# A two-layer hybrid backbone on one core: half-depth query projections first, and an expert's second step in front of its loops

## What is computed

```python
mod_x = silu(c) @ w_ada[l] + b_ada[l]            # 6 x 1024: shift, scale, gate, twice
mod_c = silu(c_ctx) @ w_ada[l] + b_ada[l]
px = (x * (1 + sc1) + sh1) @ w_in[l]             # and the same for ctx with mod_c
f, q, k, v, g = split(px)                        # 256, 512, 512, 512, 512 columns
mix = concat(fourier_mix(f), diff_attention(rope(q), rope(k), v), chunk_sgu(g))
x = layernorm(ALPHA * x + g1 * (mix @ w_out[l]))
hx = x * (1 + sc2) + sh2
gates = route(hx)                                # 2 of 16 experts for each token
y = sum over e: gates[e] * ((silu(hx @ w1[e]) * (hx @ w3[e])) @ w2[e])
x = layernorm(ALPHA * x + g2 * y)
```

## Time and profile before

| what | value |
|---|---|
| median of 3 runs | 1263.22 us (1261.59 to 1272.76) |
| the profiled execution | 1269.81 us, span of its instructions 1268.0 us |
| mean granted TensorE clock | 0.908 of full |
| TensorE busy | 1025.1 us, 81% of the span |
| DVE, ACT, POOL busy | 336.0, 227.2, 257.6 us |
| moved by DMA | 331.40 MB, mean 261 GB/s |
| waits of `up` for expert weights | 64.9 us |
| of the chain of waits | PE 66%, DMA 16%, issue 9% |

### The profile page before, as it was taken

One profiled execution on the slowest core, in us unless ns is written; L12 is line 12 of the kernel. 1 busy time (PEld: TensorE's weight loads), 2 busy tenths in 40 slices (PEclk: granted clock), 3 DMA queues, 4 the chain that ended last, 5 costly groups with the idle time before them and its releaser, 6 DMA issues.

```text
span 1268.0 us, 24266 instructions
## 1 busy us (share of the span) xinstructions
PE 1025.1 (81%) x9133; PEld 567.7 (45%) x9134; DVE 336.0 (26%) x787; ACT 227.2 (18%) x559; POOL 257.6 (20%) x483
## 2 busy tenths in 40 slices
PE   4999998899999989978775769998997748745860
PEld 1544756444645545544342434555444425423430
DVE  1002217423433212111110146116233201110114
ACT  0211117501411101101010123116122001100100
POOL 1000000100064333332221320000001313312431
PEclk9799999899899999998797859999997879988995
DMA  9993310380647666688999997321876999999952
GB/s 297 407 409 143 133 67 1 120 312 1 265 168 268 235 230 236 232 309 331 350 361 401 387 367 271 115 84 67 300 315 246 370 404 399 381 391 406 387 189 101
DMA packets 91140, 331.40 MB, mean 261 GB/s; under 512 B 12828, under 2 KB 15068, under 8 KB 66516
## 3 DMA queue, kind: packets, MB, share of 16 engines
q1 hardware_dynamic: 68532, 282.13, 58.4%
q0 software_dynamic: 21088, 47.48, 10.7%
q10 hardware_dynamic: 1472, 1.12, 0.3%
HBM read 303.17 MB, written 27.53 MB: 261 GB/s over the span
## 4 chain that ended last, share of the span: by engine, by line
PE 66%; DMA 16%; issue 9%; DVE 4%; ACT 3%; SPq 2%; POOL 0%; POOLq 0%; DVEq 0%; ACTq 0%
PE PS L1632 18%; PE PS L1434 17%; DMA W<-in_moe_w 13%; PE PS L1648 8%; PE PS L1551 7%; PE PS L1380 3%; PE PS L1622 3%; PE PS L1399 2%; DMA W<-in_w_ada 2%; PE PS L1640 2%; PE PS L1601 1%; ACT EX L789 1%; DMA H<-y_rows,DEST 1%; PE PS L1370 1%; PE PS L1562 1%
## 5 line engine op out<-in xcount | busy, mean ns | idle before, releaser
L1632 PE MATMUL PS<-W,EX 128*32 128x256 f32 x4224 | 280.4, 422 | 114.3 <-DMA W<-in_moe_w 64.9
L1632 PEld LDWEIGHTS PS<-W,EX 128*32 128x32 f32 x4224 | 151.3, 121 | 222.2 <-issue 153.3
L1434 PE MATMUL PS<-W,XT 128*128 128x512 f32 (+1 forms) x544 | 219.8, 565 | 3.1 <-ACT XT L722 3.1
L1434 PEld LDWEIGHTS PS<-W,XT 128*128 128x128 f32 x544 | 104.4, 194 | 112.7 <-issue 110.3
L1648 PE MATMUL PS<-W,AT 128*32 128x256 f32 x2112 | 131.0, 389 | 1.5 <-DVE AT L1267 1.5
L692 ACT ACTIVATE AT<-EX 64x512 f32<-64x512 f32 x64 | 40.4, 631 | 446.8 <-PE PS L1622 442.5
L1260 DVE COPY EX<-PS 128x256 f32<-128x256 f32 x66 | 28.0, 425 | 342.7 <-PE PS L1632 342.7
L588 POOL TENSOR_TENSOR RSTD<-VAR,HALF 128x1 f32<-128x1 f32 (+1 forms) x24 | 16.3, 683 | 482.1 <-DVE VAR L968 482.1
L619 POOL DMA_DIRECT2D y_rows<-AT x136 | 67.5, 499 | 207.9 <-DVE AT L1270 198.2
L619 POOL DMA_DIRECT2D y_rows<-EX x128 | 63.5, 496 | 166.2 <-DVE EX L1270 145.7
L1551 PE MATMUL PS<-W,XT 128*128 128x512 f32 x192 | 85.0, 603 | 0.0
(11 more groups left out here) (192 smaller groups left out, 842.3 us busy)
## 6 DMA issues: line engine op xcount, KB each, us to landing
W<-in_moe_w SPq DMA_DIRECT2D x96, 2048.0 KB, 14.1
W<-in_w_ada SPq DMA_DIRECT2D x24, 2048.0 KB, 14.6
W<-in_w_in SPq DMA_DIRECT2D x8, 2048.0 KB, 26.4
EX<-xg_rows POOLq DMA_DIRECT2D x136, 64.0 KB, 5.8
W<-in_w_out SPq DMA_DIRECT2D x4, 2048.0 KB, 9.9
xg_rows<-X POOLq DMA_DIRECT2D x1, 6656.0 KB, 30.9
y_rows<-X POOLq DMA_DIRECT2D x1, 4608.0 KB, 44.2
y_rows<-AT POOLq DMA_DIRECT2D x136, 32.0 KB, 5.2
```

The lines of the kernel that those rows point to most:

```text
L1434: mm = pe.matmul(ps[:, 0:cw], XT[:, k, P * t:P * t + P], w[:, k, :], start=(k == 0), stop=(k == KD - 1))
L1632: mm = pe.matmul(UP_PS[o:o + ROWS, 0:256], rows, moe_up(3 * p + n)[:, k, 256 * a:256 * a + 256], start=(k == 0), stop=(k == KD - 1), tile_ ...
```

## The change

It has two parts.

**The opening of layer 0.** The order of the transfers becomes: layer norm vectors, `c` and `c_ctx` as rows beside them, constants, biases, X, modulation chunks 0 and 2, the first half (in depth) of the query weights, chunks 1 and 3, the second half, and then the key weights and the rest as before. TensorE turns `c` and `c_ctx` together with the layer norm vectors. Chunks 0 and 2 are shift and scale of the first 512 of the 1024 model columns; with them the first halves of the tiles are transposed and modulated, and each query tile is begun with four of its eight matmuls (`q_half(t, 0)`), its bank staying open. Chunks 1 and 3 come between these, then the second halves of the tiles, and the last four matmuls of each query tile. Fourier group weights and SGU transposes move behind the key tiles. POOL waits for chunk 3 before it loads the small parameters and fills the tables, and ScalarE's two router loads move behind its modulation. Layer 1 keeps its order but takes its chunks as 0, 2, 1, 3.

**The expert's second step.** `rest` and `up` for the second step are written out once in front of the two loops, and the loops, which begin at the third step, are entered only if there are more than 64 rows.

```diff
+def opening():
+    ...
+    return [ada(0), ada(2), col(0), col(2), h(0, 0), h(1, 0), q(0), h(2, 0), q(1), h(3, 0), ada(1), q(2), ada(3), col(1),
+            ("at", 0), q(3), ("at", 2), col(3), h(0, 1), ("at", 5), h(1, 1), h(2, 1), ("at", 2), h(3, 1)] + \
+        [("k", 0, t) for t in range(4)]
...
+                if key == ("ada", 0, 1):
+                    q = ("in", 0, "q")
+                    sp.dma_start(slot(q)[:, 0:KD // 2, :], w_src[q][0].rearrange("(k p) n -> p k n", p=P)[:, 0:KD // 2, :])\
+                        .then_inc(q_first_in, 16)
...
+            full(pool, ("ada", 0, 3))
             params(0)
...
+                def q_half(t, hf):
+
+                    q = ("q", L, t)
+                    read(pe, ("hT", L, t, hf))
+                    if hf:
+                        w, (b, _) = weights(("in", L, "q")), BANK[q]
+                        ps, done = PS[:, b, :], bank_full[b]
+                    else:
+                        pe.wait_ge(q_first_in, 16)
+                        w = slot(("in", L, "q"))
+                        ps, done = claim(q)
+                    for k in range(4 * hf, 4 * hf + 4):
+                        mm = pe.matmul(ps, XT[:, k, P * t:P * t + P], w[:, k, :], start=(k == 0), stop=(k == KD - 1))
+                    if hf:
+                        mm.then_inc(done, 1)
...
+                    def again(j):
+                        pe.wait_ge(xgt_ready[L], step + j + 1)
+                        up(p)
+                        rest(p, step + j, p, own)
+
                     with pe.If(cnt > ROWS):
-                        with pe.Fori(0, T) as g:
-                            with pe.If(cnt > g * (4 * ROWS) + ROWS):
-                                with pe.Fori(0, 4) as i:
-                                    with pe.If(cnt > g * (4 * ROWS) + i * ROWS + ROWS):
-                                        j = 4 * g + i
...
+                        again(1)
+                        with pe.If(cnt > 2 * ROWS):
+                            with pe.Fori(0, T) as g:
+                                with pe.If(cnt > g * (4 * ROWS) + 2 * ROWS):
+                                    with pe.Fori(0, 4) as i:
+                                        with pe.If(cnt > g * (4 * ROWS) + i * ROWS + 2 * ROWS):
+                                            again(4 * g + i + 2)
```

More of the change, by code:

```diff
@@ L79, in val @@
     return sum(COUNTS[name](l) for l in range(L)) + i + 1
+FIRST = [0, 2, 1, 3]
+ORDER = FIRST + list(range(4, 12))
 def is_row(c):
@@ L116, in ada @@
         return out + mod_jobs(L, cs[-1])
-    jobs = [("lnc", L), ("ab", L), ("swT", L)] if L == 0 else []
-    jobs += ada([0, 1, 2, 3])
-    for job in first_jobs(L):
-        jobs += [job + (hf,) for hf in range(2)] if job[0] == "hT" else [job]
-    jobs += [("ab", L), ("swT", L)] if L else []
+    if L == 0:
+        jobs = [("lnc", L)] + opening()
+    else:
+        jobs = ada(FIRST)
+        for job in first_jobs(L):
+            jobs += [job + (hf,) for hf in range(2)] if job[0] == "hT" else [job]
+    jobs += [("ab", L), ("swT", L)]
     for name, _, _, n in CHUNKS[2:4]:
@@ L169, in make_plan @@
                 continue
+            if key[0] == "at":
+                n += (key[1] - n) % 8
+                continue
             if key[0] == "even":
@@ L197, in ring_plan @@
     for L in range(DEPTH):
-        for c in range(4):
+        for c in FIRST:
             put(("ada", L, c))
@@ L934, in ada_copy @@
                 ps = full(dve, key)
-                if c_ >= 2:
-                    full(dve, mod_jobs(L, c_ - 2)[-1])
-                dve.tensor_copy(R4[:, c_ % 2, :], ps).then_inc(freed(key), 1)
+                n = ORDER.index(c_)
+                if n >= 2:
+                    full(dve, mod_jobs(L, ORDER[n - 2])[-1])
+                dve.tensor_copy(R4[:, n % 2, :], ps).then_inc(freed(key), 1)
             def columns(L, c_):
@@ L1017, in group_weights @@
                 dve.tensor_copy(SWT[:, :, :].rearrange("p a b -> p (a b)"), full(dve, key)).then_inc(freed(key), 1)
-            key = ("lnc", 0)
-            dve.tensor_copy(LNC[:, :, :, :, :].rearrange("p a l j k -> p (a l j k)"), full(dve, key)[:, 0:4 * DEPTH * KD])\
-                .then_inc(freed(key), 1)
-            group_weights(0)
-            ada_copy(0, 0)
-            for c_ in range(1, 4):
-                ada_copy(0, c_)
-                columns(0, c_ - 1)
-            columns(0, 3)
+            for pair in (FIRST[0:2], FIRST[2:4]):
+                for c_ in pair:
+                    ada_copy(0, c_)
+                for c_ in pair:
+                    columns(0, c_)
             for L in range(DEPTH):
@@ L1338, in _ @@
                     if t == 0 and L + 1 < DEPTH:
-                        for c_ in range(4):
+                        for c_ in FIRST:
                             columns(L + 1, c_)
@@ L1369, in spread, with ada_product @@
                     a = CAT["sel"][0] + r
-                    pe.matmul(ps, C[:, a:a + 1].to_broadcast([P, P]), R4[:, c_ % 2, :], start=True, stop=True)\
+                    pe.matmul(ps, C[:, a:a + 1].to_broadcast([P, P]), R4[:, ORDER.index(c_) % 2, :], start=True, stop=True)\
                         .then_inc(done, 1)
+            def ada_product(L, c_):
+                ps, done = claim(("ada", L, c_))
+                w = weights(("ada", L, c_))
+                row = IDENT[0:12 * DEPTH, 12 * L + c_:12 * L + c_ + 1].to_broadcast([12 * DEPTH, 32])
+                for k in range(KD):
+                    a = 32 * (k % 4)
+                    mm = pe.matmul(ps[a:a + 32, :], CT[:, k, :], w[:, k, :], start=(k < 4), stop=False,
+                                   tile_position=(0, a))
+                for j in range(4):
+                    a = 32 * j
+                    mm = pe.matmul(ps[a:a + 32, P * j:P * j + P], row, BA[:, P * j:P * j + P],
+                                   start=False, stop=True, tile_position=(0, a))
+                mm.then_inc(done, 1)
             def ada_product(L, c_):
```

117 lines of the change are left out of this document (74 added, 43 removed).

## The result

The changed kernel takes **1254.93 us** (median of 15 runs, 1252.96 to 1260.96). The kernel before took 1263.22 us on the same chip. The ratio is 0.9926, 95% interval 0.9905 to 0.9948. That is 9.3 us less; the two medians differ by 8.3. The forecast was 1248 us, 15 less than before. The profiled execution took 1256.38 us, of which 1254.4 is the span.

The account below looks back on a forecast made before the run. The prediction took TensorE (66% of the chain) and DMA (16%) as the bound, with 9% issue. Opening 0, layer 0 -9 and layer 1 -6 gave -15 us, hence 1248 us, range 1236 to 1263.

Parts of the forecast that it names:

- the opening: Start of layer 0 to end of keys: first query matmul ten us earlier, but 10.5 us moved behind it; 0 us, -4 to +4.
- layer 0: Layer 0's experts: first half 7.8 us later, second half limited by weight loads; -9 us, between -3 and -13.
- layer 1: Layer 1's experts: loads bound up to expert 5, then cheaper exits behind two-step experts; -6 us, between -2 and -9.
- I give both together 2 to 4 us: Opening's queue: gain from removing four-byte column loads of c and c_ctx and delaying POOL's parameter loads, 2 to 4 us.
- They cost nothing: Opening: POOL's two row-table fills, some 20 us later, are first waited for behind the whole attention, so cost nothing.
- ladder of gaps: Idle ahead of the next expert's first `up`, layer 0: none after two steps, about 4.0, 3.2, 2.4 after three, four, five.
- the third rival, "the weights take it all": Experts: TensorE's saved time becomes waiting from expert 7 on, layer 1 gives 3 us; 1259 us, chance 0.24.
- The loop outgrows its store: Expert loop: longer code no longer stays in the instruction store, each jump back reloads; +37 us, 1300 us, chance 0.06.
- The exit cost stays: Expert exits: idle is the long jump, not empty rounds; +8 us layer 0, +2 layer 1, 1273 us, chance 0.07.
- The rule on fetching: Expert loop: skill's two-page fetch window weighed against its 128 KiB for TensorE; trace said to favour the larger store; no size.

Follow-up runs that it names:

- kernels with counted loops: Changed kernel or kernel before, expert loops replaced by one loop with register-held round count: 1221.97 us (new opening), 1225.75 us (second step also in front), 1225.17 us (old opening).
- kernel with looped experts alone: Changed kernel, but experts 0 and 15 of each layer keep the old loops; only the 14 between have the second step in front: 1242.77 us, ratio 0.9826.
- kernel with counted loops and a step in front: New opening and loops with register-held round count, plus the second step written out ahead of the loop in all experts: 1225.75 us, ratio 0.9687.

## Why the prediction came out as it did

**The total** lies within the range, but that is partly luck. Of its three terms the opening was put at nothing and gave 5 us, layer 0 gave half of its 9, and layer 1 gave nothing of its 6: the first error hid much of the other two. The range, 1236 to 1263, also reached up to the time of the kernel before (1263.22), so that it hardly told a gain from none.

**The opening: forecast 0, measured about -5.** Work moved behind the first query matmul was sized well: 69.3 us forecast, 68.7 measured. What failed is the step "I give both together 2 to 4 us" for the queue. The tokens' 2 MB should have moved the first modulation product from 19.75 to 25.2 us (one load, 5.5 us); it started at 18.37, so the freed queue was worth 6.9 us. Two experiments account for it: 1.6 for the columns, 5.4 for GpSimd's small loads. The second product started at 23.70, where 26.5 to 28.5 were forecast, and the first query matmul came at 33.2 in place of 38. And the halves themselves, for which the part is named, hold only 1 to 4 us: once X is early, all transposes hide behind the weights, and whole projections do nearly as well. Before, eight transposes stood between the first query tiles, with TensorE otherwise never idle.

"They cost nothing", said of the fills, was right for this change and only because of the wait on GpSimd's queue. Without that line the kernel was 12 us slower than before, mostly by the fills (14.7 of the 20.1 us that the opening lost), and the forecast had no such rival.

**Layer 0: forecast -9, measured -7.7 at expert 15 and -4.7 at layer 1; perhaps 3 stayed.** (The step alone gave -2.9 in the total, with nothing from layer 1. Layer 0 took 344.7 and 350.2 us in the two profiles with the old loops and 336.3 to 342.5 in the seven with the second step in front as in the change, so each of these sizes is good to some 5 us.) The ladder of gaps was right: nothing behind two steps, 0.8 more behind the others, expert 6 reached 8.3 us later (7.8 forecast), the transfers then at 391 GB/s (377 used). The forecast stopped at expert 15. From there to layer 1 it lost 3.0 again: a stall of 6.5 us at the last `down`, and behind it modulation weights that land when they land. The kernels with counted loops speak against the stall as the cause: without it the weights are waited for, and the stretch is no shorter (265.3 us against 261.5). This is the third rival, "the weights take it all", one stage further on.

**Layer 1: forecast -6, measured +1.5.** (The three profiles with the old loops in this layer span 251.1 to 253.8, the changed kernel took 252.6: no change that can be told.) This step failed for a reason that stood in no term and no rival: the new code stands between an expert with one step and its successor. Before the change the first jump behind expert 0 cost 0.24 us, now 5.22, and 2.12 and 2.46 follow. With experts 0 and 15 left as they were the layer takes 244.7 us: -6.4 to before. The gaps were priced about rightly: from expert 2 on the change won 3.7 us, and that kernel 5.8. The first jump over twice the code was priced at nothing, and it cost 5.1 by expert 2. Which block a jump can still reach without a fetch is not settled by these runs: in the kernel with looped experts alone, the last `down` of layer 0 had 3.79 us of "issue" with the same code at expert 15 that cost 0.74 before, and the kernel with the step in layer 0 only had 3.02 us ahead of expert 1 of layer 1, where the same code had cost 0.24.

**The rivals.** *The loop outgrows its store*: no fetch in the loop in the changed kernel, so it was rightly small; the third step in front went over the edge. *The exit cost stays*: false, the gap behind two steps is gone. I read the ladder as the price of empty rounds, and the counted loops bear it out: with no empty round no gap is left, 19 us in the first six experts. They take away the outer loop and the tests as well; how much each part of the nest costs was not split further.

**The rule on fetching.** In the rows a first jump over the further steps goes with a stall (5.22 us, and five blocks were fetched from 955 to 985 us; that the fetch is what TensorE waits for is inferred from this), and a loop stays at hand until a third step is written out. The Trainium skill ("Runtime: NRT & Kernel Launch", Instruction fetch mechanics) says that a taken branch to a page outside the window of two forces a fetch; the trace agrees as to the stall, and not as to two pages. Its 128 KiB for TensorE, eight blocks of 16 KiB, are not contradicted: from 345 to 470 us the changed kernel fetched 8 blocks and up to 690 us no more, the kernel with the third step in front fetched 10 and then 18 more. Some of these blocks are expert 0's and not the loop's, so the runs do not measure where the store ends.

## What to carry to other kernels

Count empty rounds before writing steps out: where the number of rounds is in a register, a loop with that bound removed the whole gap (-42 us), while code written in front of the loop moved it (-3 us) and cost 5 us in layer 1, where it was jumped over for the first time. Ask of each block of code who has to jump over it, and for the first time. When a transfer is moved to the front, look for what waits for it alone on another queue: it starts too, and here the fills would have cost the opening some 15 us had they not been held back.

## What the runs showed of the hardware

- A loop whose bound is in a register costs no more per round than one with a constant: 6.51 us from `up` to `up` with it, 6.52 before.
- A first forward jump over two steps of code went with 5 to 7 us of standing still where it lands (5.22, 6.00, 4.28 + 2.26), over one step with 0.2 to 4 us (0.24, 0.17, 3.02, 3.79; the 0.24 was followed by 4.57 one part later). In the kernel with counted loops and a step in front, the stall in layer 1 cost 5.5 us and the one at the end of layer 0, ahead of late weights, none.
- The loop of the changed kernel ran without instruction fetches from 470 to 690 us, and the one with a further step did not (18 blocks from 470 to 670 us): 25 us in layer 0. In layer 1 that code fetched again too, but took 249.7 us from expert 0 to 15, no more than before.
- Under 1 MB of small loads on GpSimd's queue (q0 moved 0.79 MB in the first 60 us, 0.46 with them held back) delayed the first modulation product by 5.4 us, about as long as a whole load of 2 MB takes (5.5 in the kernel before).
